# Ends of attention pairs inside the next slot, reciprocal rows and rotations by transfer, and the causal mask in bias rows

## The reference

```python
h = rmsnorm_2(x, norm_g[layer]);  u = h @ w_in[layer]
(qa, ka, va, fa, za, qb, kb, vb, zb, qc, kc, vc, zc, ga, gb, gc) = split(u)
log_f = log_sigmoid(fa + b_forget)
ya = forgetting_attention(qa, ka, va, log_f) * silu(za)        # 4 heads, causal, bias c[t] - c[s], c = cumsum(log_f)
yb = dilated_mixture_attention(rope(qb), rope(kb), vb) * silu(zb)   # 6 heads
yc = banded_attention(rope(qc), rope(kc), vc, 127, sinks) * silu(zc) # 6 query heads, 2 key heads
merged = sigmoid(ga) * (ya @ w_br_a) + sigmoid(gb) * (yb @ w_br_b) + sigmoid(gc) * (yc @ w_br_c)
x = x + merged @ w_out
```

## Time and profile before

| | |
|---|---|
| median of 3 runs | 3653.48 us |
| the profiled execution | 3650.48 us |
| its span, first to last instruction | 3648.7 us |
| TensorE matmul busy | 3466.6 us, 95% |
| DVE, GpSimd, ACT busy | 1841.1, 1178.4, 776.0 us |
| mean granted TensorE clock | 0.981 of 2.4 GHz |

### The profile page before, as it was taken

How to read it: one execution, slowest core, us unless ns; L and a number is a source line. 1 busy time by engine, 2 the same in 40 slices (tenths; PEclk the granted TensorE clock), 3 DMA queues, 4 the chain that set the end, 5 groups by cost and what they waited for, 6 DMA issues and landing times.

```text
span 3648.7 us, 55929 instructions
## 1 busy us (share of the span) xinstructions
PE 3466.6 (95%) x22924; PEld 2790.0 (76%) x22924; DVE 1841.1 (50%) x2497; ACT 776.0 (21%) x1210; POOL 1178.4 (32%) x557
## 2 busy tenths in 40 slices
PE   5999699999999999989999999999999999999997
PEld 4888499788888888867777678888877677688886
DVE  6531566646676676753444544433534444534434
ACT  3311433211101101232222320000322232300001
POOL 2334054233344343421112223434322212244342
PEclk9999799999999999999999999999999999999998
DMA  2111000121111111121000011111310000111111
GB/s 110 53 68 46 0 4 4 51 86 47 51 46 48 50 46 52 64 94 35 24 23 29 30 72 50 46 52 46 123 41 24 29 23 24 54 62 48 50 46 64
DMA packets 40958, 174.60 MB, mean 48 GB/s; under 512 B 4576, under 2 KB 5088, under 8 KB 39536
## 3 DMA queue, kind: packets, MB, share of 16 engines
q1 hardware_dynamic: 36432, 135.85, 11.4%
q10 hardware_dynamic: 4384, 36.64, 2.7%
HBM read 157.73 MB, written 14.75 MB: 47 GB/s over the span
## 4 chain that ended last, share of the span: by engine, by line
PE 89%; DVE 7%; issue 1%; ACT 1%; DMA 1%; POOL 0%; DVEq 0%; ACTq 0%; SPq 0%; POOLq 0%
PE ps L451 53%; PE ps L887 10%; PE ps L1256 5%; PE ps L1064 3%; PE ps L1095 3%; PE ps L717 3%; PE ps L1113 3%; DVE sc L2444 1%; PE ps L1025 1%; PE ps L915 1%; PE ps L1134 1%; PE ps L1017 1%; DVE sq_sum L1813 1%; PE ps L1070 1%; PE ps L470 0%
## 5 line engine op out<-in xcount | busy, mean ns | idle before, releaser
L349 POOL TENSOR_TENSOR wH<-wraw,pv 128x1024 fp32r<-128x1024 f32 x239 | 460.0, 1925 | 2215.0 <-PE ps L451 1814.2
L451 PE MATMUL ps<-hH,wH 128*128 128x512 f32 x2800 | 882.0, 396 | 20.6 <-issue 13.3
L451 PE MATMUL ps<-hH,wL 128*128 128x512 f32 x2800 | 869.4, 392 | 0.0
L451 PE MATMUL ps<-hL,wH 128*128 128x512 f32 x2800 | 869.3, 392 | 0.0
L451 PEld LDWEIGHTS ps<-hH,wH 128*128 128x128 f32 x2800 | 522.9, 189 | 140.8 <-issue 29.6
L351 POOL TENSOR_TENSOR wL<-wraw,wH 128x1024 fp32r<-128x1024 f32 x239 | 615.3, 2574 | 18.8
L451 PEld LDWEIGHTS ps<-hL,wH 128*128 128x128 f32 x2800 | 526.1, 189 | 110.6
L451 PEld LDWEIGHTS ps<-hH,wL 128*128 128x128 f32 x2800 | 525.0, 189 | 109.2
L2259 DVE TENSOR_TENSOR xT<-ps,xT 128x512 f32<-128x512 f32 x560 | 372.2, 689 | 11.1 <-PE ps L915 11.0
L2537 DVE TENSOR_TENSOR sg<-ps,mrows 128x1024 f32<-128x1024 f32 x46 | 56.3, 1225 | 371.7 <-PE ps L451 371.7
L1694 ACT ACTIVATE sc<-sc,stat 128x256 f32<-128x256 f32 (+7 forms) x256 | 170.9, 668 | 131.8 <-DVE stat L2451 63.4
(11 more groups left out here) (388 smaller groups left out, 4295.9 us busy)
## 6 DMA issues: line engine op xcount, KB each, us to landing
wraw<-ws SPq DMA_DIRECT2D x242, 512.0 KB, 3.5
park<-xT ACTq DMA_DIRECT2D x2, 4096.0 KB, 14.0
xT<-park ACTq DMA_DIRECT2D x2, 4096.0 KB, 12.2
xT<-xin SPq DMA_DIRECT2D x1, 4096.0 KB, 12.2
xT<-xin ACTq DMA_DIRECT2D x1, 4096.0 KB, 12.2
cBs<-out ACTq DMA_DIRECT2D x8, 512.0 KB, 4.8
out<-xT SPq DMA_DIRECT2D x8, 512.0 KB, 3.5
ed<-park ACTq DMA_DIRECT2D x4, 512.0 KB, 6.6
```

What stands on the lines that cost most here:

```text
L349: pool.tensor_tensor(wH[:, j, :], wraw[:, j, :], zero, ALU.add).then_inc(w_hi, 1)
L451: mm = pe.matmul(pair(p)[:, half * HALF:(half + 1) * HALF], wp, hp[:, k, half * HALF:(half + 1) * HALF], start=(m == 0 and n == 0), stop=( ...
```

## The change

- **Pair ends.** `rows` and the last `values` no longer stand behind period 7. `pair_end` gives a table for the first slot of what comes next (the next pair, the window keys or merge): the second transposes of block 7 after step 2, `values(7)` and one transpose of the 16 reciprocal columns after step 7. The waits for `at_y` move from before the second slot to before the value transposes (A, B), behind both slots (window) or before the rotation (C). C pairs are unrolled on TensorE.
- **Reciprocal rows by transfer.** ACT copies the transposed 16 x 128 out of PSUM, stores them in DRAM, waits, and spreads them with two DMAs over 64 partitions each into `qP`; DVE's output waits for that.
- **Mask in bias rows.** `cBs` becomes two buffers `cM[0]`, `cM[1]`. The bias rows are spread with alternate blocks of 128, four DMAs a pair instead of two. DVE puts the mask into the other blocks (`mask_bias`), ACT copies bare blocks over masked ones as they are passed (`unmask`), and the mask matmuls go.
- **Half swaps by transfer.** In B and for the window's keys, four DMAs of ACT from SBUF to SBUF swap the halves of 32 partitions in place of `rotate`. The sign goes into the sine table; C's `rotate` stays with a permutation without signs.
- Some semaphores are merged.

```diff
+            def pair_end(br, L, i, first):
+                _, transposes, values, _ = steps(br, L, i, first)
+                def values_and_rows():
+                    values(7)
+                    pe.wait_ge(sem("at_rec"), L * 8 + i + (first + 1))
+                    pe.transpose(bank(4)[0:16, 0:P], stat[:, S_REC, :], ident).then_inc(sem("at_rows"), 1)
+                return {2: lambda: transposes(7, 1), 7: values_and_rows}
...
-                        col_gemm(*slots[0], p=0)
-
-                        pe.wait_ge(sem("at_y"), pi + 1)
+                        col_gemm(*slots[0], p=0, between=ended)
                         col_gemm(*slots[1], p=1)
                         pe.wait_ge(sem("a_raw"), raw + 1)
-                        if br == "B":
-                            rotate(2, qraw2)
-                        col_gemm(*slots[2], p=0, between={5: rotate_k} if br == "B" else {})
+                        col_gemm(*slots[2], p=0)
...
-                    if br == "A":
-                        for j in range(2):
-                            pe.matmul(outs[j][:, c1 - P:c1], ident, cst[:, C_NEG, :], start=False, stop=True
-                                      ).then_inc(sem("at_S"), 1)
...
-                rows()
-                values(7)
...
                     def rotate_q():
                         pe.wait_ge(sem("a_raw"), L * 14 + i + 12)
+                        pe.wait_ge(sem("at_y"), pi + 1)
...
-                    pe.wait_ge(sem("at_y"), L * 8 + 9)
+                    pe.wait_ge(sem("at_max"), L * 128 + 130)
+                col_gemm(*next(slots), between=(pair_end("C", L, 2, 5) if first else {}) |
...
+            def swap_halves(raw, q, a_raw):
+
+                act.wait_ge(sem("a_raw"), a_raw)
+                for a in range(4):
+                    b = a ^ 1
+                    act.dma_start(SC[1][32 * a:32 * a + 32, q, :], raw[32 * b:32 * b + 32, :]).then_inc(sem("a_rot"), 16)
...
-                            spread(cBs[:, j, :], out[2 * i + j:2 * i + j + 1, L, :], L + 3)
+                            for q in range(2):
+                                spread(alternate(cM[q][:, j, :], 1 - q),
+                                       alternate(out[2 * i + j:2 * i + j + 1, L, :], 1 - q), L + 3)
...
+                def unmask(n):
+
+                    b = slice(n * P, (n + 1) * P)
+                    act.activation(cM[n % 2][:, :, b], cM[1 - n % 2][:, :, b], ACT.Copy).then_inc(sem("bB_copied"), 1)
...
+                act.wait_ge(sem("at_rows"), pi + 1)
+                act.activation(rec_rows[:, :], bank(4)[0:16, 0:P], ACT.Copy).then_inc(sem("rec_copied"), 1)
+                act.wait_ge(sem("rec_copied"), pi + 1)
+                act.dma_start(out[0:1, 4:6, :].rearrange("o k (r q) -> (o k r) q", q=P), rec_rows[:, :]
+                              ).then_inc(sem("rec_kept"), 16)
+                act.wait_ge(sem("rec_kept"), pi * 16 + 16)
+                for j in range(2):
+                    act.dma_start(qP[64 * j:64 * j + 64, :], out[0:1, 4 + j, :].to_broadcast([64, T])
+                                  ).then_inc(sem("rec_spread"), 16)
                 act.wait_ge(sem("at_y"), pi + 2)
...
+                def mask_bias():
+
+                    dve.wait_ge(sem("bB_ready"), 128 + (L * 2 + i + 1) * 64)
+                    for q in range(2):
+                        masked, bare = [rows[:, :, :].rearrange("p j (b e t) -> p e j b t", e=2, t=P)[:, q]
+                                        for rows in (cM[q], cM[1 - q])]
+                        dve.tensor_tensor(masked, bare, cst[:, C_NEG, :].unsqueeze(1).unsqueeze(1).to_broadcast([P, 2, KT // 2, P]),
+                                          ALU.subtract).then_inc(sem("bias_masked"), 1)
...
-                    dve.wait_ge(sem("at_rows"), pi + 1)
+                    dve.wait_ge(sem("rec_spread"), pi * 32 + 32)
                     dve.wait_ge(sem("a_z"), pi * 2 + 2)
-                    st.on(dve.tensor_tensor(sz[:, :], pair(1), sz[:, :], ALU.mult))
+                    st.on(dve.tensor_tensor(sz[:, :], qP[:, :], sz[:, :], ALU.mult))
```

More of the change, by code:

```diff
@@ L1038, in window_keys, with steps @@
                 pe.wait_ge(sem("at_max"), pi * 16 + 1)
[L1039 to L1040 removed]
+                col_gemm(0, u, between=pair_end("B", L, 2, 2))
                 col_gemm(1, u)
                 pe.wait_ge(sem("a_raw"), L * 14 + 11)
[L1043 removed]
+                pe.wait_ge(sem("at_y"), pi + 1)
                 pe.wait_ge(sem("a_v"), L * 6 + 6)
                 value_transposes(3)
[L1047 removed]
+            def steps(br, L, i, first):
                 pi = L * 8 + i + first
[L1049 removed]
+                last, done = pi * 16, copies(br, L, i, first)
                 def scores(n):
@@ L1091, in transposes @@
                             pe.wait_ge(sem("at_pt0"), done + n + 1)
-                        out, b = pair(0 if n == 7 and j else 2), 0
+                        out, b = pair(1 if n == 7 and j else 2), 0
                     pe.wait_ge(sem("at_exp"), last + 2 * n + j + 1)
@@ L1122, in period, with head_pair @@
                         values(n - 1)
-                    transposes(n, 1)
+                    if n < 7:
+                        transposes(n, 1)
                     if br != "C" and n == 3:
                         scores(n + 1)
[L1127 to L1140, removed]
+                return scores, transposes, values, period
+            def pair_end(br, L, i, first):
[5 more added lines that the diff above has]
+                return {2: lambda: transposes(7, 1), 7: values_and_rows}
+            def head_pair(br, L, i, first, ended={}):
+                pi = L * 8 + i + first
+                last = pi * 16
+                scores, transposes, values, period = steps(br, L, i, first)
+                pe.wait_ge(sem("at_max"), last + (2 if br == "C" else 1))
                 if br == "C":
                     u = L * (LAYER_SLOTS // 2) + i + ((SLOT_LAYER + SLOT_WINDOW) // 2 + 1)
-                    col_gemm(0, u)
+                    col_gemm(0, u, between=ended)
                     def rotate_q():
                         pe.wait_ge(sem("a_raw"), L * 14 + i + 12)
+                        pe.wait_ge(sem("at_y"), pi + 1)
                         pe.wait_ge(sem("a_vtok"), L * 6 + 6)
@@ L1224, in merge_tile, with residual_rows @@
                 pe.wait_ge(sem("sg_raw"), D8 * 3 + 1)
+                def residual_rows():
+                    pe.wait_ge(sem("rec_copied"), 8)
+                    factor_rows(2, factors(R_R1))
                 if first:
-                    pe.wait_ge(sem("at_y"), L * 8 + 9)
-                col_gemm(*next(slots), between={10: lambda: factor_rows(2, factors(R_R1))} if first and L == 0 else {})
+                    pe.wait_ge(sem("at_max"), L * 128 + 130)
+                col_gemm(*next(slots), between=(pair_end("C", L, 2, 5) if first else {}) |
+                         ({20: residual_rows} if first and L == 0 else {}))
                 if last:
@@ L2373, in forget_gates, with rope @@
                                        ).then_inc(sem("gate_rows"), 1)
-            def rope(L, n, a_raw, p, raw, dst):
+            def rope(L, n, a_raw, turned, source, rot, raw, dst):
                 step = n * 2 + (L + 1) * 2
@@ L2414, in head_pair @@
                 if br == "B":
-                    rope(L, L * 10 + i * 2, L * 14 + i * 2 + (2 * first + 1), 2, qraw2, qP)
-                    rope(L, L * 10 + i * 2 + 1, L * 14 + i * 2 + (2 * first + 2), 3, kraw2, kP)
+                    for q, raw, dst in ((0, qraw2, qP), (1, kraw2, kP)):
+                        rope(L, L * 10 + i * 2 + q, L * 14 + i * 2 + (2 * first + 1 + q), swaps(L, i * 2 + (q + 1)),
+                             SC[1][:, q, :], SC[1][:, q, :], raw, dst)
                 if br == "C":
-                    rope(L, L * 10 + i + 7, L * 14 + i + 12, 3, qraw2, qP)
-                else:
+                    rope(L, L * 10 + i + 7, L * 14 + i + 12, swaps(L, 7, i + 1), pair(3), qraw2[:, :], qraw2, qP)
+                def mask_bias():
[5 more added lines that the diff above has]
+                                          ALU.subtract).then_inc(sem("bias_masked"), 1)
+                if br == "A" and i:
+                    mask_bias()
+                if br != "C":
                     value_copy(2, L * 6 + i + first)
+                if br == "A" and not i:
+                    mask_bias()
                 def maxima(n):
```

88 lines of the change are left out of this document (53 added, 35 removed).

## The result

The changed kernel takes 3627.33 us (median of four runs, 3625.86 to 3635.39) against 3655.36 for the kernel before on the same chip (3650.1 to 3659.04), and the ratio is 0.9929, with a 95% interval of 0.9909 to 0.9949. (Ratios and intervals come from the single runs, and differ by up to 0.0006 from the quotient of the two medians.) So it is faster, by 26 to 28 us. I had forecast 50. The sign is right and the size is about half. The profiled execution took 3628.67 us, its span is 3626.9, and its mean granted clock is 0.976, where it was 0.981 before.

What follows compares the result with a forecast made beforehand. TensorE work, mostly weight products, was taken to bound the kernel. Terms 16.7 + 7.2 + 20.8 + 0.8 + 17.6 - 7.8 - 11.8 + 6.5 = 50.0 us, from 3650.5 or 3653.5 to 3602 us; range 3587 to 3628.

Steps and rivals of the forecast that it cites:

- Pair ends: After A and B pairs, row matmuls replaced by one transpose: 1.67 us saved each, 16.7 us for 10 pairs.
- rotations: In six B pairs, two rotations each removed at 1.73 us: 20.8 us gain; the window's two: 0.8 us.
- B's six pairs: The six B pairs of both layers, pair ends and rotations together: 30.8 us gain.
- window and C0: Window keys and first C pair, both layers together: 4.1 us gain.
- C's ends: Ends of C0 and C1 in each layer: 1.8 us saved each, 7.2 us for four.
- B's slack of 5.5 us: B pairs and window: the first score comes late enough to leave 5.5 us slack, so the round trip costs nothing.
- The round trip in C1 and C2: Before C1's and C2's rotation TensorE waits 2.6 us for the raw copy, plus 0.3: -11.8 us, bounds -6 and -24.
- Rival (a): Clock drops behind seven or eight new waits, 1.7 us each, 13 us: total 3615 us; chance 0.15.
- A0: First A pair of each layer: longer wait for the bias, 3.9 us twice, -7.8 us, bounds -6 and -14.
- the forecast 44.6: Step from C0's reciprocal to C1's: 43.45 - 1.8 + 2.9 = 44.6 us.
- A1: Second A pair of each layer, bias ready long before its first score: 12.1 us gain over both layers.
- Merge: Slot 0 starts at once; layer 0 waits 5 us before branch products; gains 2.3 and 4.2, together 6.5 us.

Runs made afterwards that it cites:

- c_early_q: Changed kernel with C's next q copied ahead of the wait for the spread and C's rope before yL: 3597.62 us, ratio 0.9859 to the kernel before.
- a0_filler: Changed kernel with 18 unread products placed in TensorE's wait in each layer's first A pair: 3621.78 us, ratio 0.9921 to the kernel before.

## Why the prediction was right or wrong, step by step

- **Pair ends and rotations: right.** B's six pairs gained 30.5 of 30.8 us, window and C0 4.1 of 4.1, and the rotations hold alone, 20.7 by steps (20.8). That leaves 9.8 for B's six ends (10.0), which no run undid by themselves. C's ends are worth 2.08 each (1.8).
- **B's slack of 5.5 us: right.** No wait for rope or copies appeared in B's slots; the transfers are hidden there.
- **The round trip in C1 and C2, "4 x 2.9 = -11.8": this is the step that failed.** The steps came out 4.5, 3.9, 4.3 and 3.8 us longer than the forecast 44.6. The wait is 4.2 to 4.4 instead of 2.6: 0.8 us later data, and 1.26 from yL at 2.49. Behind it stand 2.3 to 3.0 us of low clock, for which the sum had nothing. The steps lost 21.1 us although the ends gained 4 x 2.08 in them, so the term is about -29, worse than my bound of -24. c_early_q removes it and finds 29.1 us in these four steps.
- **Rival (a), the clock: the mechanism was right, its chance and its price wrong.** I gave 0.15 and 1.7 us a wait, from stretches at 0.72. The stretches behind the new waits are at 0.51 to 0.69, and C's cost 3.0, 2.4, 2.9 and 2.3, A0's 2.7 and 1.0 (a0_filler). That is 14.3 us for six waits, half of the miss; merge's wait has its low clock besides. The way of pricing was sound: what the clock misses to 1.00 times the length of the stretch is 0.40 x 7.6 = 3.0 behind C1's wait and 0.34 x 6.9 = 2.3 behind C2's (3.0 and 2.4 measured). But the stretches behind the new waits are deeper and longer than those of the earlier trace rows, which stood at other starts. The Trainium skill ("TensorE: Matmul & The Clock Gate", Part 1) says that idleness throttles the array and activity releases it. The trace agrees: the 4.3 us of idleness give 0.60 behind them, and with work in the same 4.3 us it is 1.00. I had cited the rule, and should have moved it from the rivals into the sum, since the same prediction forecast waits of 3 to 5 us.
- **A0, "-7.8": the length of the wait was right, the rest not.** The spread landed 6.76 us after the first issue, 0.8 more than the 5.96 of the earlier trace rows; I had taken 0.8. DVE's two products took 2.3. The wait of 4.18 is in the range named. With the low clock behind it the mask's gain in A0 turned into a loss: -3.2 in place of +1.0. The Trainium skill ("DMA: Bandwidth & Descriptors", Specifications) has pieces of 512 bytes at line rate; the trace agrees as far as it goes, since from the last issue's end to DVE's start are 4.7 us, and 5.1 before with whole rows.
- **A1, 12.1 forecast, 9.0 measured.** Of the 3.1 us that miss, 2.1 are in layer 0. There the sixth block has a low stretch behind nearly the same wait for a maximum as before (2.30; 2.08 before): the score takes 2.53 us (1.56 before), the transposes behind it 1.33 (0.71). The other 1.0, in layer 1, I have not placed.
- **Merge: half right.** In layer 0 the wait is there and the releaser is the forecast one, 7.21 instead of 5: xT is issued 1.0 us later and DVE has it 1.7 later than its row, and the low clock follows. In layer 1 slot 0 starts with no wait, and the gain is 5.9 against 4.2, since the low stretch of the earlier trace rows is gone with it (clock 1.00 in the same place).
- **Two slips in the sum.** 4 x 2.9 is 11.6 and not 11.8, and 0.8 + 2.45 + 0.55 is 3.8 and not 3.9. Together they are 0.4 us, and change nothing.
- **The range** of 3587 to 3628 was right only at its edge (3627.33). Its upper end had added 12 for C and 6 for A0 and assumed that rival (a) fits inside; the real case was C's bound and rival (a) at once, since both come from the same wait.
- **Still open.** The 1.3 us lost ahead of the first score of layer 0, where the code is the same, and why yL takes 2.49, were not tried by themselves. In the traces of the other kernels that score stands at 1605.3 to 1608.4 us with the same code ahead of it (1605.4 before, 1606.7 in the changed kernel), so the 1.3 is within what single executions scatter. For yL the traces say more, below.

## What to carry to other kernels

A transfer in place of matmuls pays where the work behind it has slack (B, 30 us) and not where the next pair's first operand stands behind it in the same engine's queue. Put that operand's copy ahead of the wait: here it turned -21 us into +8. Each wait of about 4 us that a change puts into dense TensorE work goes into the sum at 4 and another 2 to 3 us here, unless other work can stand in it.

## What the runs showed of the hardware

**The same wait isn't always followed by a low clock.** The three B pairs of a layer do the same, yet their steps are 79.25, 77.77 and 79.20 in layer 0. TensorE's rows of the sixth block, in B0 and B1 of the changed kernel, and the stretches around them:

```profile
1790.61 2.93 PE L1073 MATMUL ps<-kP,qP 64*128 64x512 f32 x8 [2.37 <-DVE stat L2507]
...
1869.78 1.56 PE L1073 MATMUL ps<-kP,qP 64*128 64x512 f32 x8 [2.37 <-DVE stat L2507]
```
```profile
1789.00:1795.00 6.00, 4.39 (x25) 2.54 (x27) 2.54 (x10) 2.27 (x5) 0.59 (x1) 0.72 0.32 87
1867.00:1873.00 6.00, 3.63 (x36) 2.28 (x32) 3.32 (x10) 2.82 (x7) 1.76 (x1) 1.00 0.31 87
```

The wait is 2.37 us in both. In one the clock drops to a mean of 0.72 and the score takes 1.37 us more; in the other it stays at 1.00. So a wait of this length costs 0 or 1.4 us by where it happens to fall, and single pairs should not be compared to better than that. Behind the waits over 4 us that are shown here it was low each time.

**DVE beside GpSimd.** yL took 2.49 us in C1 with GpSimd's split of a weight running beside it, and 1.22 in c_early_q. The ten traces hold 160 yL, all 128 x 1024. The 44 with nothing of GpSimd beside them take 1.22 or 1.23 us. The 110 that start while GpSimd makes `wL` take 2.45 to 2.99, and always 1.07 to 1.10 more than the time that the two share, as if yL got little done until `wL` was finished. (The other six stand at merge of layer 0 beside both products of a split.) Before the change no yL fell on a split. No experiment moved GpSimd's work alone, but no yL speaks against it as the cause.

**Small transfers.** Store of 16 rows of 512 bytes, spread over 128 partitions and seen by DVE: 6.35 us (2040.15 to 2046.50), of which 1.38 is the store. The swaps of 128 KB within on-chip memory landed in a median of 2.3 us from issue.
